# Rotary half swap of two blocks on ScalarE, another order of stick-breaking's end, squares added one by one

## The reference, cut to what matters

```python
def rms_norm(x, g):
    return x * rsqrt(mean(x * x) + 1e-6) * g
def rope(t, pos):                       # half = 32, heads of 64
    t1, t2 = t[..., :half], t[..., half:]
    return concatenate([t1 * cos - t2 * sin, t2 * cos + t1 * sin])
for i in range(2):
    h = h + 0.5 * rms_norm(swiglu(rms_norm(h, g[0])), g[1])
    h = h + rms_norm(mixer_i(rms_norm(h, g[2])), g[3])
    h = h + 0.5 * rms_norm(swiglu(rms_norm(h, g[4])), g[5])
# stick-breaking: log_stay = where(visible, log_sigmoid(-z), 0)
#   log_pass = cumsum(log_stay, reverse=True) - log_stay
#   w = where(visible, exp(log_sigmoid(z) + log_pass), 0);  o = w @ v
```

## Time and profile before

| | |
|---|---|
| median of 3 runs | 1033.29 us |
| the profiled execution's own time | 1033.83 us |
| its span, first to last instruction | 1032.0 us |
| TensorE busy | 99% |
| VectorE busy | 63% |
| ScalarE busy | 51% |
| GpSimd busy | 2% |
| granted TensorE clock, mean | 0.998 |

### The profile page before, as it was taken

One profiled execution on the slowest core, in us unless ns is written; L12 is line 12 of the kernel. 1 busy time (PEld: TensorE's weight loads), 2 busy tenths in 40 slices (PEclk: granted clock), 3 DMA queues, 4 the chain that ended last, 5 costly groups with the idle time before them and its releaser, 6 DMA issues.

```text
span 1032.0 us, 19401 instructions
## 1 busy us (share of the span) xinstructions
PE 1020.8 (99%) x7724; PEld 978.1 (95%) x7724; DVE 653.0 (63%) x915; ACT 527.3 (51%) x759; POOL 16.8 (2%) x28
## 2 busy tenths in 40 slices
PE   9999999999999999999999999999999999999997
PEld 8999999999998999999999999999998999888886
DVE  5765553478775876555348765554488777876632
ACT  5643443446665564444335543443447756655433
POOL 0000000000000000000000000000014000000000
PEclk9999999999999999999999999999999999999999
DMA  8665544514333256545551654544513244655451
GB/s 329 217 231 170 188 172 164 181 63 147 141 123 105 100 205 222 185 163 166 188 177 56 239 195 168 185 177 163 179 66 124 88 159 169 243 199 186 181 184 41
DMA packets 24533, 171.25 MB, mean 166 GB/s; under 512 B 2976, under 2 KB 2976, under 8 KB 4384
## 3 DMA queue, kind: packets, MB, share of 16 engines
q1 hardware_dynamic: 24048, 169.49, 46.3%
q10 hardware_dynamic: 432, 1.00, 0.2%
HBM read 169.43 MB, written 1.05 MB: 165 GB/s over the span
## 4 chain that ended last, share of the span: by engine, by line
PE 91%; DVE 4%; DMA 2%; ACT 2%; issue 1%; SPq 0%; DVEq 0%; ACTq 0%
PE ps L1277 21%; PE ps L1279 21%; PE ps L1278 21%; PE ps L1382 7%; PE ps L1380 3%; DMA raw<-in_panels_dram 2%; PE ps L1337 2%; PE ps L1339 2%; PE ps L1349 2%; PE ps L1679 2%; PE ps L1680 2%; PE ps L1678 2%; PE ps L1612 1%; PE ps L1584 1%; PE ps L1438 1%
## 5 line engine op out<-in xcount | busy, mean ns | idle before, releaser
L556 ACT CAST w_hi<-raw 128x1024 fp32r<-128x1024 f32 x312 | 312.6, 1048 | 349.5 <-PE ps L1279 260.2
L848 DVE TENSOR_TENSOR w_lo<-raw,w_hi 128x1024 fp32r<-128x1024 f32 x312 | 370.2, 1225 | 180.8 <-ACT w_hi L556 180.0
L1277 PE MATMUL ps<-y,w_lo 128*128 128x272 f32 (+1 forms) x1150 | 335.6, 292 | 0.3 <-DVE w_lo L848 0.2
L1279 PE MATMUL ps<-y,w_hi 128*128 128x272 f32 (+1 forms) x1150 | 332.2, 289 | 0.0
L1278 PE MATMUL ps<-y,w_hi 128*128 128x272 f32 (+1 forms) x1150 | 330.6, 287 | 0.0
L1277 PEld LDWEIGHTS ps<-y,w_lo 128*128 128x128 f32 x1150 | 216.4, 188 | 2.5 <-issue 1.1
L1278 PEld LDWEIGHTS ps<-y,w_hi 128*128 128x128 f32 x1150 | 216.8, 189 | 0.2
L1279 PEld LDWEIGHTS ps<-y,w_hi 128*128 128x128 f32 x1150 | 216.4, 188 | 0.0
L1277 PE MATMUL ps<-h_hi,w_lo 128*128 (+1 forms) x528 | 152.1, 288 | 0.0
L1278 PE MATMUL ps<-h_hi,w_hi 128*128 (+1 forms) x528 | 152.0, 288 | 0.0
L1279 PE MATMUL ps<-h_lo,w_hi 128*128 (+1 forms) x528 | 151.3, 286 | 0.0
(11 more groups left out here) (203 smaller groups left out, 1237.0 us busy)
## 6 DMA issues: line engine op xcount, KB each, us to landing
raw<-in_panels_dram SPq DMA_DIRECT2D x156, 1024.0 KB, 4.8
first<-in_first_dram SPq DMA_DIRECT2D x3, 784.0 KB, 6.9
xT<-in_x_dram SPq DMA_DIRECT2D x1, 1088.0 KB, 13.6
out_dram<-fT SPq DMA_DIRECT2D x4, 256.0 KB, 2.0
const<-in_const_dram ACTq DMA_DIRECT2D x1, 920.0 KB, 10.2
first<-in_first_dram SPq DMA_DIRECT2D x2, 392.0 KB, 3.7
gain_row<-in_row_dram SPq DMA_DIRECT2D x1, 512.0 KB, 5.7
gains<-in_gains_dram ACTq DMA_DIRECT2D x1, 48.0 KB, 3.6
```

The lines of the kernel that those rows point to most:

```text
L556: nc.scalar.copy(w_hi[:, g % SLOTS, part], raw_part(g, part)).then_inc(hi_ready, 1)
L848: nc.vector.tensor_tensor(w_lo[:, g % SLOTS, part], raw_part(g, part), w_hi[:, g % SLOTS, part].bitcast(F32), ALU.subtract).then_inc(lo_re ...
L1277: nc.tensor.matmul(dst, w_lo[:, slot, pc], yh, start=first, stop=False, skip_group_check=shared)
L1279: return nc.tensor.matmul(dst, w_hi[:, slot, pc], yl, start=False, stop=last, skip_group_check=shared)
```

## The change

Sliding window: for query blocks 2 and 4 no rotation matmul is done. ScalarE copies the swapped 32-row halves of the block (`swap`, four copies of 32 x 2 x 256; block 2 in step 2 ahead of `exps(0)`, block 4 half in step 5 after `o_high(1)` and half in step 6 ahead of `o_high(2)`), GpSimd multiplies them by sin, and the sign moves from the rotation matrix into the sine table. `rotate(3)` stays. From step 7 on VectorE takes the step's first `w_lo` half after `o_low`.

Stick-breaking: the first two input tiles go to banks 6 and 7 and no longer wait for bank 0's drain; only the second waits for `pre_var`. In steps 18 to 20 TensorE does column 0, then columns 1 and 2, then the panel-0 tiles of columns 3, 4 and 5, of which 4 waits for `d_ready` 8. The rest follows in another order.

Sub-layer ends: VectorE adds tiles 1 to 5 one by one; except in the sliding-window sub-layer ScalarE squares tiles 2 and 3 one by one.

```diff
@@ -63,6 +63,8 @@
 SB_FILL = 3
+SB_EARLY = [[(0, [0, 1, 2])], [(1, [0, 1, 2]), (2, [0, 1, 2])], [(3, [0]), (4, [0]), (5, [0])]]
+SB_REST = [[(3, 1), (6, 0), (7, 0)], [(4, 1), (5, 1), (6, 1), (7, 1)], [(3, 2), (4, 2), (5, 2), (6, 2), (7, 2)]]
 SB_AT = [0, 6, 11, 16]
@@ -105,6 +107,10 @@
+SWAPPED = (2, 4)
+SWAP_ROWS = [(0, 32), (32, 0), (64, 96), (96, 64)]
@@ -187,6 +193,11 @@
+def sb_bank(n):
+    return O_BANK + n if n < 2 else n % 2
@@ -418,6 +429,7 @@
         rs_ready = sem("rs_ready")
+        swapped = sem("swapped")
         rc_ready = sem("rc_ready")
@@ -524,6 +536,11 @@
                     nc.gpsimd.memset(s[:, :, :, SW_W:], 0.0).then_inc(tail_zero, 1)
+                if b in SWAPPED:
+                    pool.wait_ge(swapped, 4 * SWAPPED.index(b) + 4)
+                    nc.gpsimd.tensor_tensor(rot_s[:, :, c0:L], rot_s[:, :, c0:L], spread(cst("sin"), 2, c0),
+                                            ALU.mult).then_inc(rs_ready, 1)
                 if b >= 2:
@@ -730,12 +747,22 @@
+                    def swap(b, n0, n):
+                        row = SW_Q + 2 * b - 2
+                        a.wait_ge(sw_drained, 2 * b + 1)
+                        a.wait_ge(roped, b)
+                        for dst, src in SWAP_ROWS[n0:n0 + n]:
+                            nc.scalar.copy(rot_s[dst:dst + 32, :, META:L],
+                                           qkv[src:src + 32, row:row + 2, META:L]).then_inc(swapped, 1)
...
                         if st == 2:
+                            swap(2, 0, 4)
                             exps(0)
@@ -756,8 +783,12 @@
                             exps(st - 2)
+                        if st == 6:
+                            swap(4, 2, 2)
                         if not early and 0 <= st - 4 < PAIRS:
                             o_high(st - 4)
+                        if st == 5:
+                            swap(4, 0, 2)
                         if st == 3:
@@ -801,9 +832,15 @@
                 for n in range(2):
+                    if n == 1 and t.kind != "swa":
+                        for d in (2, 3):
+                            a.wait_ge(f_done, KT * k + d + 1)
+                            nc.scalar.activation(sq[:, d, t0:L], out_tile(ps, t, d), ACT.Square).then_inc(f_sq, 1)
+                        save_f(n)
+                        break
                     a.wait_ge(f_done, KT * k + 2 * n + 2)
                     nc.scalar.activation(sq[:, 2 * n:2 * n + 2, t0:L], out_pair(ps, t, n), ACT.Square)\
-                        .then_inc(f_sq, 1)
+                        .then_inc(f_sq, n + 1)
                     if t.kind == "swa" and n == 0:
@@ -964,7 +1001,7 @@
                             v.wait_ge(panel_done, t.g0 + i + 1)
-                        nc.vector.tensor_tensor(qkv[:, KT * (i % 3) + 2 * (i // 3) + c, :], ps[:, c, 0:L],
+                        nc.vector.tensor_tensor(qkv[:, KT * (i % 3) + 2 * (i // 3) + c, :], ps[:, sb_bank(n), 0:L],
                                                 rms_inv[:], ALU.mult).then_inc(tile_drained, 1)
@@ -1071,8 +1108,8 @@
                         turned = ps[:, 0:2, 0:L] if b == 0 else ps[:, 5, :].rearrange("p (a n) -> p a n", a=2)
-                        v.wait_ge(rot_done, b + 1)
-                        if b >= 3:
+                        v.wait_ge(rot_done, min(b + 1, 3))
+                        if b >= 2:
                             v.wait_ge(roped, b)
@@ -1125,16 +1162,19 @@
                             normalise(st - 3)
-                        lo_halves(n0, 1)
+                        if st < SW_TILES + 1:
+                            lo_halves(n0, 1)
                         if st < SW_TILES:
...
                             rope(1)
-                        elif st in (2, 4, 6):
-                            rope(st // 2 + 1)
+                        elif st == 4:
+                            rope(3)
                         if 0 <= st - 4 < PAIRS:
                             o_low(st - 4)
+                        if st >= SW_TILES + 1:
+                            lo_halves(n0, 1)
                         if 0 <= st - 1 < PAIRS:
@@ -1187,29 +1227,25 @@
-                v.wait_ge(f_sq, 7 * k + 1)
+                v.wait_ge(f_sq, 8 * k + 1)
                 if t.kind == "ffn":
...
                                             ALU.add).then_inc(f_acc, 1)
-                v.wait_ge(f_acc, 5 * k + 1)
-                v.wait_ge(f_sq, 7 * k + 2)
-                nc.vector.tensor_tensor(sq[:, 0:2, t0:L], sq[:, 0:2, t0:L], sq[:, 2:4, t0:L],
-                                        ALU.add).then_inc(f_acc, 1)
-                for n, d in enumerate((1, 4, 5)):
-                    v.wait_ge(f_acc, 5 * k + 2 + n)
-                    if d >= 4:
-                        v.wait_ge(f_sq, 7 * k + d - 1)
+                v.wait_ge(f_acc, 6 * k + 1)
+                for d in range(1, 6):
+                    if d > 1:
+                        v.wait_ge(f_acc, 6 * k + d)
+                        v.wait_ge(f_sq, 8 * k + d)
                     nc.vector.tensor_tensor(sq[:, 0, t0:L], sq[:, 0, t0:L], sq[:, d, t0:L],
...
-                    v.wait_ge(f_sq, 7 * k + (5 if d == 6 else 7))
+                    v.wait_ge(f_sq, 8 * k + (6 if d == 6 else 8))
                     nc.vector.tensor_copy(fT[:, d, t0:L], out_tile(ps, t, d)).then_inc(f_saved2, 1)
@@ -1421,9 +1457,12 @@
                         pe.wait_ge(lo_ready, 2 * g + 2)
-                        pe.wait_ge(tile_drained, 1 if n < 2 else n + 2)
+                        if n == 1:
+                            pe.wait_ge(pre_var, t.u + 1)
+                        if n >= 2:
+                            pe.wait_ge(tile_drained, 1 if n < 4 else n + 2)
                         for k in range(KT):
-                            mm = three(ps[:, c, 0:L], g % SLOTS, 256 * k + P * c, y_hi[:, k, :], y_lo[:, k, :],
+                            mm = three(ps[:, sb_bank(n), 0:L], g % SLOTS, 256 * k + P * c, y_hi[:, k, :], y_lo[:, k, :],
                                        k == 0, k == KT - 1)
@@ -1507,18 +1546,19 @@
                     pe.wait_ge(const_in_sem, 16)
-                    pe.wait_ge(pre_var, t.u + 1)
                     for st in range(SB_TILES + SB_FILL):
...
                         else:
-                            d = st - SB_TILES
                             pe.wait_ge(lo_ready, 2 * (t.g_out + 2) + 2)
...
                             pe.wait_ge(tile_drained, SB_TILES + 3)
-                            if d == 2:
-                                pe.wait_ge(z_ready, PAIRS)
-                            out_column(d, range(3), True, False)
+                            for d, js in SB_EARLY[st - SB_TILES]:
+                                if d == 2:
+                                    pe.wait_ge(z_ready, PAIRS)
+                                elif d == 4:
+                                    pe.wait_ge(d_ready, PAIRS)
+                                out_column(d, js, True, False)
                         for g in range(GROUPS):
@@ -1552,7 +1592,7 @@
                         if b >= 2:
-                            pe.wait_ge(rs_ready, b)
+                            pe.wait_ge(rs_ready, 2)
                         for c in range(2):
@@ -1632,7 +1672,7 @@
                         elif j == 0 and n == 2:
-                            pe.wait_ge(rs_ready, 5)
+                            pe.wait_ge(rs_ready, 4)
                         elif j == 0:
@@ -1654,8 +1694,8 @@
                             rotate(1)
-                        elif st in (2, 4, 6):
-                            rotate(st // 2 + 1)
+                        elif st == 4:
+                            rotate(3)
                         if 0 <= st - 4 < PAIRS:
@@ -1740,13 +1780,13 @@
                         bank = bank_half(t)[i]
-                        pe.wait_ge(f_sq, 7 * t.u + 5)
+                        pe.wait_ge(f_sq, 8 * t.u + 6)
                         mm = nc.tensor.matmul(ps[:, bank, c0:c1], cst("ones"), sq[:, 6, c0:c1], start=True, stop=False)
...
                             mm.then_inc(panel_done, 1)
-                        pe.wait_ge(f_acc, 5 * t.u + 5)
+                        pe.wait_ge(f_acc, 6 * t.u + 6)
                         nc.tensor.matmul(ps[:, bank, c0:c1], cst("ones"), sq[:, 0, c0:c1], start=False, stop=False)
-                        pe.wait_ge(f_sq, 7 * t.u + 6 + i)
+                        pe.wait_ge(f_sq, 8 * t.u + 7 + i)
                         nc.tensor.matmul(ps[:, bank, c0:c1], cst("ones"), sq[:, 7, c0:c1],
@@ -1754,12 +1794,11 @@
                 if t.kind == "sb":
-                    pe.wait_ge(d_ready, PAIRS)
-                    for j in range(t.n_out - 1):
-                        for d in range(SB_FILL, KT):
-                            if j == 0 and d >= KT - 2:
+                    for j, rest in enumerate(SB_REST):
+                        for d, i in rest:
+                            if i == 0:
                                 pe.wait_ge(ol_ready, d + 1)
```

(6 more changed lines are left out.)

## The result

| | before | after |
|---|---|---|
| median | 1033.21 us (17 runs) | 1035.81 us (17 runs) |
| profiled execution's own time | 1033.83 us | 1035.59 us |
| its span | 1032.0 us | 1033.8 us |

The account below looks back on a forecast made before the run. TensorE, busy 1020.8 of 1032.0 us, was taken as the bound. Terms -1.1 - 0.2 - 0.1 + 0.5 = -0.9 took the profiled 1033.83 to 1032.9, less 0.5 for the median: 1032.4 us, range 1030.5 to 1034.8.

Parts of the forecast that it names:

- part 1: Sliding window: two rotations removed save 1.8 us, new waits cost 0.7, moved w_lo halves nothing; -1.1 us.
- (a): Rival, sliding window: ScalarE's queue becomes the bound, at the copies before o_high(2) in step 6; +6.2 us fully exposed, chance 0.04.
- partial case: ScalarE's queue partly exposed in the sliding window, 2 to 4 us of waits; 1033.5 to 1036, chance 0.16 shared with (b).
- part 3: Stick-breaking's end: one sp_lo wait goes, -0.75, a new wait for log_weights comes, +0.65; -0.1 us.
- Part 4: Sub-layer ends: single adds cost 0.15 us at each of sub-layers 0, 2, 3, nothing at both attentions; +0.5 us.
- Part 2: Stick-breaking's start: the first tile no longer waits for bank 0's drain; -0.2 us, between -0.4 and 0.
- (a) in full: Sliding window: all ScalarE copies and GpSimd products exposed; +6.2 us, 1039.5, chance 0.04.
- (e): Rival, whole kernel: far more TensorE idle time goes than seen, over 5.2 us; chance 0.02.
- (c): Rival, stick-breaking's end: both waits go and d_ready is in time; -1.75 us instead of -0.1, 1030.7, chance 0.10.
- (d): Rival, sub-layer ends: they cost nothing, as the sum's matmul has hidden slack; 1031.9 us, chance 0.10.
- (b): Rival, sliding window: GpSimd and VectorE hold each other off a shared port pair; +3.5 us, 1036.8; 0.16 shared, in part.

Follow-up runs that it names:

- experiment 1: Changed kernel with VectorE's w_lo halves of steps 7 to 12 back ahead of o_low; 1033.85 us, ratio 1.0007.
- experiment 2: Kernel before with only the w_lo halves of steps 7 to 12 moved behind o_low; 1037.45 us, ratio 1.0036.
- experiment 4: Kernel before with only the half swap of blocks 2 and 4 in place of their rotations; 1033.64 us, ratio 1.0000.
- experiment 5: Changed kernel with only step 7's w_lo half behind o_low, those of steps 8 to 12 ahead of it; 1032.63 us, ratio 0.9991.
- experiment 8: Kernel before with only the squares added one by one; 1033.56 us, ratio 1.0005.
- experiment 3: Changed kernel with the squares of tiles 2 and 3 paired again at all ends; 1035.47 us, ratio 1.0020.
- experiment 9: Kernel before with only the stick-breaking's first two input tiles in banks of their own; 1033.30 us, ratio 1.0000.
- experiment 11: Changed kernel with only step 7's half moved, squares paired, and two w_lo halves of stick-breaking's step 20 ahead of o_low; 1032.30 us, ratio 0.9995.

## Why the prediction was wrong

| step | forecast | in the trace | |
|---|---|---|---|
| two rotations go | -1.8 | -1.75 | right |
| new waits at scores(2), scores(6), turn(4) | +0.7 | +0.57 | near |
| w_lo halves moved | 0 | +2.5 | **wrong** |
| stick-breaking's start | -0.2 | -0.38 | undersized |
| stick-breaking's last steps | -0.1 | -0.09 | right |
| stick-breaking's sub-layer end | 0 | +0.44 | **wrong** |
| ends of sub-layers 0, 2, 3 | +0.45 | +0.59 | undersized |

**The step that failed** is one sentence of part 1: "The reordered w_lo halves from step 7 on are a step later, but their panels are used two steps later, so nothing." It asked who reads w_lo and was right on that: no product waited for one. It did not ask who waits for the half to *finish reading*: the raw slot, through it SyncE's queue, 4.9 us of load, ScalarE's cast of the next sub-layer's panel, and the squares behind that cast (2.0 of the 2.5). Nor did it ask what stands behind the half on VectorE: logits and a normalisation for which TensorE waits in step 9 (0.5). It also took "a step later" for the delay, when the half was put behind a wait for `o_high` of up to 3.15 us. Experiments 1 and 2 show it from both sides: -1.96 without the move, +4.2 (1037.45 against 1033.2) with the move alone. No rival had this mechanism. Rival (a) had the right engine, ScalarE, at the wrong place, and that 1035.8 lies within the 1033.5 to 1036 of its partial case is luck: its condition, block 4's sum far behind TensorE, cost 0.22 us.

**The second failure** cancelled itself. Part 1 credited the full 1.1, and experiments 1 and 4 show that without the moved half of step 7 a wait for `o_low(3)` takes 1.3 to 1.4 us of it back. That this part of the sum came out right is luck: the change itself cured a wait that I had not seen.

**The third** is the same omission in part 3. I counted column parts against sp_lo and log_weights, and the new wait for log_weights has the size that I worked out (0.60 more than the ordinary step from start to start, forecast 0.55 to 0.65). TensorE in the changed kernel:

```profile
321.93 0.29 PE L1315 MATMUL ps<-o_lo,w_hi 128*128 128x272 f32 x1
322.66 0.39 PE L1313 MATMUL ps<-o_hi,w_lo 128*128 128x272 f32 x1 [0.44 <-DVE fT L1038]
```

But the new order also moves the point at which the first panel's buffers are free, and nothing in the working asked for it. My premise that the 0.81 wait at running_sums(6) stays was wrong too: it is no part of either kernel's steady course. Experiment 5's profile has it, at 0.7, and the others have 0.1 there. The same goes for the start of the sum: the 0.5 by which the profiled execution of before stood above its median is about the size of this wait.

**Part 4** was too small by a quarter: 0.19 to 0.21 at each end where I took 0.15, less than the chain's own +0.2. The five adds of the changed kernel, against 0.72 and 1.40 in the earlier trace rows:

```profile
204.49 2.35 DVE L1242 TENSOR_TENSOR sq<-sq 128x272 f32<-128x272 f32 x5
...
206.89 0.38 PE L1788 MATMUL ps<-sq,const 128*128 128x136 f32 x1
```

The adds end at 206.84 and L1788 starts 0.05 later: no slack, as read. That the single adds cost nothing at the two attentions' ends held in experiment 8.

**Part 2**: the step of 0.43 has no counterpart. Each step there is 0.12 to 0.13:

```profile
227.94 0.28 PE L1314 MATMUL ps<-y,w_hi 128*128 128x272 f32 x1
228.07 0.29 PE L1315 MATMUL ps<-y,w_hi 128*128 128x272 f32 x1
```

Of the 0.38, 0.30 is that step. I kept back a third of it for the chains behind, and in the trace they didn't claim it.

**The rivals.** (a) in full and (e) did not happen. (c) is refuted by the new wait above, (d) by the +0.2 at three ends. The copies and products were priced well: groups by line after, count, busy us, mean ns:

```profile
L756 ACT COPY rot_s<-qkv 32x512 f32<-32x512 f32 x8 | 4.9, 617 | 0.2
...
L542 POOL TENSOR_TENSOR rot_s<-rot_s,const 128x512 f32<-128x512 f32 x2 | 2.6, 1299 | 6.0 <-ACT rot_s L756 6.0
```

(b) is seen once on TensorE's path. VectorE and GpSimd in the changed kernel:

```profile
807.43 0.70 DVE L1141 TENSOR_TENSOR den<-tot,snk 128x4 f32<-128x4 f32 x1
```

```profile
806.83 1.28 POOL L547 TENSOR_TENSOR qkv<-rot_s,rot_c 128x512 f32<-128x512 f32 x1
```

An addition of four elements per partition took 0.70 us and ended with GpSimd's sum, at 808.1. The normalisation behind it was late for turn(4) by 0.24 us, where I had put 0.1. The Trainium skill (SBUF — State Buffer, Who interferes with whom) gives the rule of one holder at a time. By that rule the second waits out the first, and this row agrees; it was right to count this in tenths and not as the rival's 3.5 us.

## What to carry to other kernels

When an instruction is moved on an in-order queue, follow both of its ends: who needs its result, and who needs its inputs' buffers back, through the loads behind them to whatever is queued behind those loads' first readers, also across the boundary of a stage. Look at what it is put behind: behind a wait, the delay is the wait's length, not one instruction. Look at what it is put ahead of: that is late by its whole length. When time is taken from the bound engine, name the result that is next in line at each later step, since a gain of 1.75 us was worth nothing until that one was moved too.

## What was unexpected of the hardware

The same 4-element addition took 0.16 us without a GpSimd instruction beside it and 0.70 beside one. In experiment 1's timeline both stand within 5 us:

```profile
806.87 0.70 DVE L1141 TENSOR_TENSOR den<-tot,snk 128x4 f32<-128x4 f32 x1
...
811.45 0.16 DVE L1141 TENSOR_TENSOR den<-tot,snk 128x4 f32<-128x4 f32 x1
```

TensorE's clock, too, differs between executions that wait alike. Behind an idle stretch of 1.66 us it was granted at 1.2 GHz from 838.0 to 841.3 (experiment 3), and behind one of 1.65 us, in the changed kernel, it stayed at 2.4. In experiment 2's profile it was at 1.2 GHz from 343.4 to 346.7, behind the wait of 2.2 us, and stayed at 2.4 behind the later one of 1.8 us. So such a wait of the bound engine can cost more than its length, in experiment 3's profile 1.1 us more.

From execution to execution, the profiled runs differ by up to 1.4 us at the first products (shift +1.08, +1.28, 0.00 and -0.12 in the changed kernel and experiments 4, 9 and 11, none of which alters that place) and by 0.7 at one wait of the stick-breaking. An edit worth 0.4 us is seen in a comparison of landmarks and not in medians of 11 runs, whose ratios have intervals of 0.1% to either side.
